# A mixture-of-experts block whose one weight buffer in the arena is loaded behind attention, with tile 0 routed and gathered ahead of tile 1

## The reference

```
t  = moba_attention(x)                       # 8 heads of 128, with a relative bias
h1 = layer_norm(ALPHA * x + t, ln_g[0], ln_b[0])
logits = h1 @ w_router + b_router            # 32 experts
top_logit, top_e = top_k(logits, 4); gate = softmax(top_logit)
for each expert e, for the tokens that chose it:
    g, u = split(h1[tokens] @ w_gate_up[e] + b_gate_up[e])      # 1024 -> 2 x 1024
    act  = min(g, 7) * sigmoid(1.702 * min(g, 7)) * (clip(u, -7, 7) + 1)
    y[tokens] += gate * (act @ w_down[e] + b_down[e])           # 1024 -> 1024
x = layer_norm(ALPHA * h1 + y, ln_g[1], ln_b[1])
```

## Time and profile before

| | us |
|---|---|
| median of 3 runs (lowest, highest) | 1375.93 (1375.58, 1377.43) |
| the profiled execution, its own time | 1376.69 |
| its span | 1374.9 |
| mean granted clock of TensorE, share of full | 0.994 |
| TensorE busy | 1330.1 (97%) |
| VectorE, ScalarE, GpSimd busy | 441.2, 346.9, 49.6 |
| bytes moved by DMA | 484.17 MB, mean 352 GB/s |

### The profile page before, as it was taken

The page is one execution under the profiler, slowest core; times in us unless marked ns, Lnnn a source line. Parts: engine busy times, 40 slices in busy tenths (PEclk is TensorE's granted clock), DMA queues, the critical chain, the costliest instruction groups (busy, mean ns, idle before and its releaser), DMA issues.

```text
span 1374.9 us, 17056 instructions
## 1 busy us (share of the span) xinstructions
PE 1330.1 (97%) x7358; PEld 718.6 (52%) x7358; DVE 441.2 (32%) x746; ACT 346.9 (25%) x576; POOL 49.6 (4%) x60
## 2 busy tenths in 40 slices
PE   9999999999999999969999999999999999999997
PEld 7996333333333333323333333333336998999986
DVE  5565121112111111101211111111107776888854
ACT  4541011101101110100110101100116545666642
POOL 2010000000000000000000000000002000022200
PEclk9999999999999999989999999999999999999999
DMA  9968999999999999999999999999996444265530
GB/s 378 376 233 359 428 421 430 430 432 429 430 431 430 430 431 429 431 429 430 431 432 429 432 429 431 429 431 430 432 427 242 153 154 153 87 254 183 184 123 31
DMA packets 44378, 484.17 MB, mean 352 GB/s; under 512 B 4780, under 2 KB 4832, under 8 KB 13712
## 3 DMA queue, kind: packets, MB, share of 16 engines
q1 hardware_dynamic: 42432, 477.63, 83.4%
q0 software_dynamic: 1872, 5.44, 1.1%
HBM read 481.99 MB, written 1.06 MB: 351 GB/s over the span
## 4 chain that ended last, share of the span: by engine, by line
PE 78%; DMA 15%; DVE 4%; issue 1%; ACT 1%; DVEq 0%; SPq 0%; ACTq 0%
PE bank L835 25%; PE bank L641 19%; PE bank L843 13%; DMA ring<-in_moe_w_gate_up 12%; PE bank L1143 4%; PE bank L855 3%; PE bank L808 3%; PE bank L624 3%; DMA ring<-in_w_in 2%; PE bank L827 2%; PE bank L751 2%; PE bank L1079 1%; PE bank L1029 1%; DMA arena<-in_x_by_feature 1%; DVE w_split L1552 1%
## 5 line engine op out<-in xcount | busy, mean ns | idle before, releaser
L835 PE MATMUL bank<-ring,arena 128*64 128x512 f32 x2048 | 448.9, 594 | 9.8 <-DMA ring<-in_moe_w_gate_up 9.8
L835 PEld LDWEIGHTS bank<-ring,arena 128*64 128x64 f32 x2048 | 143.2, 137 | 313.2 <-issue 290.3
L1750 DVE TENSOR_SCALAR arena<-bank 128x512 f32<-128x512 f32 x32 | 22.1, 692 | 654.8 <-PE bank L835 654.7
L843 PE MATMUL bank<-ring,arena 128*64 128x512 f32 x1008 | 223.5, 595 | 1.8 <-DMA ring<-in_moe_w_down 1.3
L641 PE MATMUL bank<-x_hi,w_split 128*128 128x256 f32 x1056 | 195.2, 285 | 2.1 <-DVE x_lo L1559 2.1
L641 PEld LDWEIGHTS bank<-x_hi,w_split 128*128 128x128 f32 x1056 | 167.2, 193 | 2.6 <-DVE x_lo L1559 1.5
L1552 DVE TENSOR_TENSOR w_split<-ring,w_split 128x2048 fp32r<-128x2048 f32 x61 | 139.5, 2289 | 60.4 <-ACT w_split L1198 60.2
L641 PE MATMUL bank<-x_lo,w_split 128*128 128x256 f32 x528 | 150.1, 284 | 0.0
L1299 ACT ACTIVATE arena<-arena 128x512 f32<-128x512 f32 x32 | 20.2, 630 | 495.3 <-DVE arena L1750 495.3
L843 PEld LDWEIGHTS bank<-ring,arena 128*64 128x64 f32 x1008 | 69.8, 137 | 135.3 <-issue 126.4
L1198 ACT CAST w_split<-ring 128x2048 fp32r<-128x2048 f32 x62 | 118.2, 1910 | 74.2 <-PE bank L641 42.5
(11 more groups left out here) (288 smaller groups left out, 1102.1 us busy)
## 6 DMA issues: line engine op xcount, KB each, us to landing
ring<-in_moe_w_gate_up SPq DMA_DIRECT2D x128, 2048.0 KB, 34.5
ring<-in_moe_w_down SPq DMA_DIRECT2D x63, 2048.0 KB, 34.1
ring<-in_ffn_w_up SPq DMA_DIRECT2D x22, 1024.0 KB, 4.8
ring<-in_w_in SPq DMA_DIRECT2D x14, 1024.0 KB, 8.0
ring<-in_ffn_w_down SPq DMA_DIRECT2D x11, 1024.0 KB, 4.9
ring<-in_a_w_in SPq DMA_DIRECT2D x10, 1024.0 KB, 20.9
ring<-in_a_w_out SPq DMA_DIRECT2D x2, 2048.0 KB, 14.0
ring<-in_w_out SPq DMA_DIRECT2D x4, 1024.0 KB, 5.0
```

The lines of the kernel that those rows point to most:

```text
L835: last = mm(bank[q // 2][half * 64:half * 64 + 64, :], chunk(xeT, c), w[:, c % 2, q * 512:(q + 1) * 512], start=False, stop=c == KC - 1)
L843: last = mm(bank[3][half * 64:half * 64 + 64, :], chunk(actT, c), w[:, c % 4, half * 512:(half + 1) * 512], start=c == 0, stop=c == KC - 1)
```

## The change

- SyncE issues piece 10 (`SPARE`) behind `o_ps` (attention's last product), ahead of the last four ring pieces, and no longer behind the norm.
- For that, the first norm's gain and offset move: `row_g0` to 13612, loaded by GpSimd right behind the relative bias; `row_b0` to 6144 (the place of attention's v), loaded behind `o_ps`, ahead of the router's weights. `bias_sel` moves to 13548, the output projection's fourth bank from 0 to 7, logits and ranks to banks 4 and 5.
- The norm's last step is done in two halves of 512 columns, each with its own `h1_ready`.
- TensorE computes tile 0's ranks as soon as tile 0 is chosen; VectorE makes tile 0's places and selection behind the PSUM copy of tile 1; TensorE gathers tile 0's half for expert 0 (`gather_first(0)`) behind tile 1's logits, and tile 1's half when its selection is ready.
- `add_bias` for expert 0 stands behind tile 0's logits, the tables stand behind the first gate-up piece of expert 0.
- Fillers: one pair of 512 columns more at tile 0, none at tile 1, and pairs of 256 columns (`fill`) in place of 512 around ranks and gather.

The diff, cut to its core:

```diff
@@ -162,7 +162,9 @@
...
         LEVEL_BANKS = (4, 6, 7, 4, 5, 6, 7, 4)
-        OUT_BANKS = (4, 6, 5, 0)
+        OUT_BANKS = (4, 6, 5, 7)
+        LOGITS = [bank[4][:, t * N_EXP:(t + 1) * N_EXP] for t in range(NT)]
+        RANKS = [bank[5][:, t * N_EXP:(t + 1) * N_EXP] for t in range(NT)]
         OUT_ORDER = (3, 0, 1, 2)
@@ -174,6 +176,7 @@
...
         moments = at(13542, NT, 2)
+        row_g0, row_b0 = at(13612, D), at(6144, D)
         row_g = at(8192, D)
@@ -189,7 +192,7 @@
...
         selgT = at(3456, NT, P)
-        bias_sel = at(3712, CAP)
+        bias_sel = at(13548, CAP)
         actT = at(6144, 4, P)
@@ -499,13 +502,13 @@
...
                 load_piece(A_OUT[g])
+            sp.wait_ge(o_ps, PAIRS)
+            load_piece(SPARE)
             for k, q in enumerate(OUT_ORDER):
...
             first_late = PIECES_E * (EXTRA_AFTER + 1)
-            sp.wait_ge(h1_ready, NT)
-            load_piece(SPARE)
             for n in range(SPARE + 1, first_late):
@@ -575,11 +578,10 @@
...
-            pool.wait_ge(max_ready, H)
-            pool.dma_start(row_g, row(ln_g[0, :], D)).then_inc(ln0_in, 16)
-            pool.dma_start(row_b, row(ln_b[0, :], D)).then_inc(ln0_in, 16)
+            pool.dma_start(row_g0, row(ln_g[0, :], D)).then_inc(rel_in, 16)
             pool.wait_ge(pt_ps, H)
             pool.wait_ge(o_ps, PAIRS)
+            pool.dma_start(row_b0, row(ln_b[0, :], D)).then_inc(ln0_in, 16)
             pool.dma_start(wr, w_router.rearrange("(c p) e -> p c e", p=P)).then_inc(moe_small_in, 16)
@@ -773,33 +775,60 @@
...
             before = const("before")
+            def add_bias():
...
+            def gather_first(t):
+                for half in range(2):
+                    last = mm(bank[2][half * 64:half * 64 + 64, :], sel[:, t, :], h1[:, t, half * 512:(half + 1) * 512],
+                              start=t == 0, stop=t == NT - 1)
+                return last
+            def fill():
+                mm(bank[3][:, 0:T], ident, cst[:, 0:T], start=True, stop=True)
             for t in range(NT):
-                pe.wait_ge(h1_ready, t + 1)
                 for g in range(2):
+                    pe.wait_ge(h1_ready, 2 * t + g + 1)
                     b = 4 + 2 * t + g
...
                 if t:
+                    pe.wait_ge(chosen_ready, 1)
+                    mm(RANKS[0], before, chosen[:, 0, :], start=True, stop=True).then_inc(rank_ps, 1)
+                    pe.wait_ge(h1T_dve, 1)
+                else:
                     repeat(3, 1)
-                    pe.wait_ge(h1T_dve, 1)
+                    pe.wait_ge(moe_small_in, 6 * 16)
                 pe.wait_ge(h1T_act, 2 + t)
-                if t == 0:
-                    pe.wait_ge(moe_small_in, 6 * 16)
                 for c in range(KC):
-                    last = mm(bank[1 + t][:, 0:N_EXP], h1T[:, c, t * P:(t + 1) * P], wr[:, c, :],
+                    last = mm(LOGITS[t], h1T[:, c, t * P:(t + 1) * P], wr[:, c, :],
                               start=c == 0, stop=c == KC - 1)
...
                 if t == 0:
+                    pe.wait_ge(bsel_ready, 1)
+                    add_bias()
                     repeat(3, 1)
-            pe.wait_ge(chosen_ready, 1)
-            mm(bank[0][:, 0:N_EXP], before, chosen[:, 0, :], start=True, stop=True)
-            mm(bank[0][:, N_EXP:2 * N_EXP], ones, chosen[:, 0, :], start=True, stop=False)
-            repeat(3, 1)
+            pe.wait_ge(sel_ready, 1)
+            gather_first(0)
+            mm(RANKS[1], ones, chosen[:, 0, :], start=True, stop=False)
+            fill()
             pe.wait_ge(chosen_ready, 2)
-            mm(bank[0][:, N_EXP:2 * N_EXP], before, chosen[:, 1, :], start=False, stop=True).then_inc(rank_ps, 1)
-            repeat(3, 1)
+            mm(RANKS[1], before, chosen[:, 1, :], start=False, stop=True).then_inc(rank_ps, 1)
+            fill()
+            pe.wait_ge(sel_ready, 2)
+            gather_first(1).then_inc(xe_ps, 1)
+            fill()
@@ -856,18 +878,20 @@
...
-            pe.wait_ge(sel_ready, 1)
-            gather().then_inc(xe_ps, 1)
...
             pe.wait_ge(xe_ready, 1)
             turn_chunks(2, xe, 2).then_inc(xeT_ps, 1)
+            fill()
+            def tables():
+                pe.wait_ge(gates_ready, 1)
+                for t in range(NT):
+                    turn(bank[3][0:N_EXP, t * P:(t + 1) * P], gates[:, t, :])
+                for t in range(NT):
+                    turn(bank[3][0:N_EXP, T + t * P:T + (t + 1) * P], place[:, t, :])
+                for t in range(NT):
+                    last = mm(bank[4][0:N_EXP, 0:1], chosen[:, t, :], ones[:, 0:1], start=t == 0, stop=t == NT - 1)
+                last.then_inc(table_ps, 1)
@@ -878,15 +902,17 @@
...
             for i in range(N_EXP):
-                pe.wait_ge(bsel_ready, i + 1)
                 if i:
+                    pe.wait_ge(bsel_ready, i + 1)
                     pe.wait_ge(selgT_ready, i)
-                add_bias()
+                    add_bias()
                 pe.wait_ge(xeT_ready, i + 1)
...
                     gate_up(s, buffer_of(n, 2)).then_inc(piece_done, 1)
+                    if i == 0 and s == 0:
+                        tables()
@@ -900,7 +926,7 @@
...
                 if i + 1 < N_EXP and not pause:
-                    pe.wait_ge(sel_ready, i + 2)
+                    pe.wait_ge(sel_ready, i + 3)
                     gather().then_inc(xe_ps, 1)
@@ -1649,12 +1675,12 @@
...
-            dve.wait_ge(ln0_in, 32)
+            dve.wait_ge(rel_in, 80)
             dve.wait_ge(x_in, 32)
...
                 dve.wait_ge(logit_ps, t + 1)
-                link(tt(logit[:, t, :], bank[1 + t][:, 0:N_EXP], br, ALU.add))
+                link(tt(logit[:, t, :], LOGITS[t], br, ALU.add))
                 link(dve.max(top8[:, t, :], logit[:, t, :]))
@@ -1666,6 +1692,10 @@
...
+            def select_bias(i):
+                ts(bias_sel, ones[:, 0:CAP], const("own")[:, i:i + 1], None, ALU.mult).then_inc(bsel_ready, 1)
+            select_bias(0)
             for t in range(NT):
@@ -1675,23 +1705,31 @@
...
                 root_of(t, moments[:, t, 1:2], 1.0, LN_EPS)
-                link(stt(h1[:, t, :], h1[:, t, :], moments[:, t, 0:1], row_g, ALU.subtract, ALU.mult))
+                link(stt(h1[:, t, :], h1[:, t, :], moments[:, t, 0:1], row_g0, ALU.subtract, ALU.mult))
                 r = refine(t)
-                stt(h1[:, t, :], h1[:, t, :], r, row_b, ALU.mult, ALU.add).then_inc(h1_ready, 1)
+                dve.wait_ge(ln0_in, 16)
+                for g in range(2):
+                    cols = slice(g * 512, (g + 1) * 512)
+                    stt(h1[:, t, cols], h1[:, t, cols], r, row_b0[:, cols], ALU.mult, ALU.add).then_inc(h1_ready, 1)
+            places = const("slot")
+            def first_places(t):
+                dve.wait_ge(rank_ps, t + 1)
+                link(stt(place[:, t, :], RANKS[t], 0.5, chosen[:, t, :], ALU.add, ALU.mult))
+                ts(sel[:, t, :], places[:, 0:CAP], place[:, t, 0:1], None, ALU.is_equal).then_inc(sel_ready, 1)
             choose(0)
...
             dve.tensor_copy(h1T[:, 4:8, P:T], bank[7][:, :].rearrange("p (c n) -> p c n", c=4)).then_inc(h1T_dve, 1)
+            first_places(0)
             choose(1)
             dve.wait_ge(chosen_ready, 2)
-            places = const("slot")
+            first_places(1)
...
                    place[:, :, i:i + 1].to_broadcast([P, NT, CAP]), ALU.is_equal).then_inc(sel_ready, 1)
@@ -1699,10 +1737,6 @@
...
-            dve.wait_ge(rank_ps, 1)
-            link(stt(place.rearrange("p t e -> p (t e)"), bank[0][:, 0:2 * N_EXP], 0.5,
-                chosen.rearrange("p t e -> p (t e)"), ALU.add, ALU.mult))
-            select(0)
             dve.wait_ge(gexp_ready, 1)
@@ -1710,7 +1744,6 @@
...
             dve.wait_ge(gates_ready, 1)
-            select_bias(0)
```

23 lines of the change are left out of this document (6 added, 17 removed).

## The result

The changed kernel takes 1384.37 us (median of 4 runs, 1382.78 to 1384.98), beside 1375.76 (4 runs, 1375.56 to 1377.43) of the kernel before: ratio 1.0059, 95% interval 1.0044 to 1.0074. By the medians it is 8.6 us slower, where 1.7 us faster was forecast.

What follows compares the result with a forecast made beforehand. The expert weights' DMA stream bounds the kernel. Queue 3.8 us earlier, release 1.55 plus 0.16; the smaller, 1.7, decides: 1375.93 becomes 1374.2 us, eight in ten 1372.4 to 1376.2.

Steps and rivals of the forecast that it cites:

- Part 3: Small loads after attention: router's weights and expert biases land 0.6 to 1.8 us later, by 112 at most, in time.
- The rival of the clock: TensorE, 122 to 131 us: thinned fillers let its clock fall, 1.75 us per fall; two falls give 1377.7; chance 0.07.
- Part 2: Routing chain: expert 0 starts at 130.8, 1.55 us earlier, so the first recycled piece is released at 134.4.
- From there on the stream is as before: Weight stream behind the first recycled piece: continues unchanged, and all later stages follow it, 1.7 us earlier.
- The forecast's own rule: First recycled piece: starts when both queue (3.8 us earlier) and release (1.55 us earlier, plus 0.16) let it.
- the forecast's 1.7: Whole kernel: gain from the earlier release, 1.55 us plus 0.16 us lost before, the smaller of the two limits.
- 4.88 us, 134.4 + 4.88 = 139.3: in time: Second recycled piece: issued at 138.6, before it must follow the first by 4.88 us.
- The hole filled: Weight stream, 108 to 112 us: the arena's piece, 4.88 us of transfer, goes into the 5.0 us hole.
- The queue alone decides: Rival at the first recycled piece: the arena's piece held the stream; moving it gains 3.8 us, 1372.1; chance 0.13.
- Hidden anyway: Rival in the experts' stage: TensorE sets its end; only 0.8 us come out, 1375.1, or nothing, 1375.9; chance 0.15.
- the room of 2.9 us: VectorE before tile 1's second half arrives at 115.6: 2.9 us in hand, so row_b0 costs nothing until 112.8.
- The rival on row_b0: Norm's offset load lands after 112.8 and delays tile 1's norm; 3.5 us later gives 1376.3; chance 0.02.

Runs made afterwards that it cites:

- 1: Changed kernel, with SyncE issuing the arena's piece only when the router's weights, router's bias and expert biases have landed; 1375.91 us, ratio 0.9999.
- 2: Changed kernel with the arena's piece issued behind the second norm again, as before the change; 1376.01 us, ratio 1.0012.
- 3: Changed kernel with row_b0, router's weights and bias and expert biases issued on SyncE's queue ahead of the arena's piece, instead of by GpSimd; 1376.83 us, ratio 1.0005.
- 9: Changed kernel with the expert biases and router's bias issued early, behind the first norm's scale; arena's piece still at 100 us; 1376.61 us, ratio 1.0005.
- 11: Changed kernel with the five weight pieces behind attention each loaded as four transfers of 4 KB per partition instead of one of 16 KB; 1376.47 us, ratio 1.0006.
- 5: Kernel before with only the arena's piece moved behind attention's last output pair, and the first norm's rows in their new places; 1382.82 us, ratio 1.0046.
- the seventh: Kernel of 1 (arena's piece waits for the small loads) with one filler more behind tile 1's transposes; 1375.88 us, ratio 1.0001.
- 14: Changed kernel with expert 1's down-projection pieces 10 and 11 used in the other order; 1385.12 us, ratio 1.0076.
- the twelfth: Kernel before with expert 1's down-projection pieces 10 and 11 used in the other order; 1377.6 us over 11 runs, ratio 1.0032.
- The fourth: Changed kernel with nine filler pairs instead of one ahead of TensorE's wait for the small loads; 1382.02 us, ratio 1.0048.
- the sixth: Changed kernel with five fillers instead of one ahead of TensorE's wait for the small loads; 1382.32 us, ratio 1.0039.
- the eighteenth: Changed kernel with five fillers ahead of the wait for the small loads and one more behind tile 1's transposes; 1381.83 us, ratio 1.0034.
- 8: Kernel of the seventh with the tables behind the third piece of expert 0 instead of the first; 1375.72 us, ratio 0.9997.
- 10: Kernel of 9 with one filler more behind tile 1's transposes and the tables behind expert 0's third piece; 1375.61 us, ratio 0.9996.
- 13: Kernel of 10 with expert 1's down-projection pieces 10 and 11 used in the other order; 1374.17 us over 11 runs, ratio 0.9987.
- 16: Kernel of 10 without expert 0's scatter products, so its output lacks the first expert; 1374.94 us, ratio 0.9991.
- 17: The twelfth's kernel, unchanged, run again on another occasion; 1376.02 us, ratio 1.0004.
- the fifteenth: Kernel before without expert 0's scatter products, so its output lacks the first expert; 1375.80 us, ratio 1.0002.

## Why the prediction was wrong

**The step that failed** is in Part 3: "The router's weights and the expert biases move back by 0.6 to 1.8 us to at most 112". I priced a wait of the issuing engine and took the landing from the earlier trace rows as it was. But that load of 6.9 us, and those of before (8.0 and 7.3), stood beside a single piece; the hole from 108 to 112, which I filled with weights, was the time in which the small loads got through. Beside a full queue they took 12.7 to 17.3 us, and the last landed at 120.9, not at 112. Experiments 1, 2, 3, 9 and 11 each take away the meeting of the two, in five ways, and each gives the 8 us back; 5 brings it about alone. That the queues take turns packet by packet is what the counts of 11 bear out. The Trainium skill (DMA: Bandwidth & Descriptors, "Queues, rings and completion order") says that each DMA engine goes round the queues that have work one whole packet at a time; the counts (177 to 174, 241 to 246) agree. I read the page for its fit of one load and passed over this rule, which spoke against the change.

**What the late landing cost**, by comparison with the seventh, which has the same order, no wait and a full clock: logits at 120.96 instead of 117.50, 3.5 us; from logits to expert 0 18.06 instead of 13.79, 4.3 us of halved clock; against that the new order's own gain, 131.29 instead of 132.28, 1.0 us. 3.5 + 4.3 - 1.0 = 6.7 (rounded). The rival of the clock, which had 0.07, so carries more than half; but I had it fall by thinned fillers, and here it fell behind a stop. All three profiles with such a stop (the changed kernel, 5 and 14; 3.7 to 5.2 us) have 0.50 behind it. The clock also falls without one: 0.50 at 126 to 128 in the first and second experiments, with no wait of TensorE above 0.3 us. Thinned fillers are not shown as the cause, since 3, 9 and 11 have the same order and kept 1.00, and the twelfth fell with before's fillers. The fourth, at full clock, bears the second share out with 13.63 us; the sixth and the eighteenth, which should have given the whole sum, did not keep the clock up.

**The release (Part 2) was nearly right, and what follows it was not.** With clock and loads in order expert 0 starts at 131.05 to 131.3 (experiments 7, 8, 10, 11 and 13; forecast 130.8), and the recycled piece goes out at 134.7 to 135.0 (134.4), 1.0 to 1.2 us sooner than before and not 1.55. The end should have come 1.7 us sooner. The second wrong step is "From there on the stream is as before": the forecast itself had TensorE only 0.8 us ahead behind the tables, and took it that the next release would be in time all the same.

Three times from each profile (expert 0's first matmul, an issue looked at below, the end of in_w_in) and the bytes that SyncE's queue moved from 95 to 150 us, put against before at 430 GB/s:

| kernel | expert 0 | issue | difference | MB | ahead by 150 us | in_w_in landed | ahead there |
|---|---|---|---|---|---|---|---|
| before | 132.28 | 186.48 | 54.20 | 18.43 | | 1031.59 | |
| changed | 139.02 | 194.13 | 55.11 | 15.47 | -6.9 | 1039.15 | -7.6 |
| 1 | 132.70 | 187.81 | 55.11 | 18.22 | -0.5 | 1032.78 | -1.2 |
| 5 | 138.79 | 192.99 | 54.20 | 15.78 | -6.2 | 1037.85 | -6.3 |
| 7 | 131.29 | 186.40 | 55.11 | 18.30 | -0.3 | 1032.23 | -0.6 |
| 8 | 131.05 | 186.16 | 55.11 | 18.35 | -0.2 | 1032.09 | -0.5 |
| 10 | 131.16 | 186.26 | 55.10 | 19.06 | +1.5 | 1030.54 | +1.1 |
| 11 | 131.09 | 186.20 | 55.11 | 18.56 | +0.3 | 1033.91 | -2.3 |
| 13 | 131.25 | 182.93 | 51.68 | 19.06 | +1.5 | 1030.46 | +1.1 |
| 18 | 136.94 | 192.04 | 55.10 | 16.19 | -5.2 | 1036.94 | -5.4 |

What the stream has won or lost by 150 us is there at its end, within 0.7 us in this table but for the eleventh, which loses 2 us more between 184 and 204 us (the fourth and sixth, not in the table, lose 1.2 more). Why, I cannot explain. The forecast's own rule is that the later of queue and release decides. By it three cases come out, from one profile each:

- **The queue still decides** (7 and 8): the arena's piece waits for the small loads, the hole at 110 us stays, the DMA share is 0.9 or more from 114 to 144 us, and an earlier release finds the queue full. That fits the eighth's tables giving nothing.
- **The release decides** (10, 13 and 16): the hole is filled, the recycled piece goes out 1.0 to 1.1 us sooner, and in_w_in lands 0.9 to 1.1 us sooner. This is what is left of the forecast's 1.7.
- **The second release decides** (3 and 9, the change as planned but for the small loads): with the tables between the first two pieces the second recycled piece is issued 4.3 us behind the first, not 3.4 as in before and the tenth. With the 1.6 taken off, the ninth's in_w_in lands 1.3 us later than the tenth's, though expert 0 starts at the same time. The filler is the only other edit between them, and the clock is 1.00 in both there; the tables were not moved alone with the hole filled. In the forecast this step was "4.88 us, 134.4 + 4.88 = 139.3: in time".

**A place that looks like a bound and is not shown to be one.** Of expert 1's last two pieces the arena's gives no slot back, so the load into piece 11's slot waits until TensorE has used both. Before, its issue, the next one, and the stretch:
```profile
186.48 0.33 SPq L489 DMA_DIRECT2D ring<-in_moe_w_gate_up  x1
191.08 0.33 SPq L489 DMA_DIRECT2D ring<-in_moe_w_down  x1
```
```profile
186.00:188.00 2.00, 2.00 (x16) 0.54 (x14) 0.00 (x0) 0.58 (x1) 0.00 (x0) 1.00 0.94 301
```
SyncE's queue runs dry there (0.13 MB at 188 to 190 us). I took this load for what sets the end: the changed kernel's is 7.65 us late and its in_w_in 7.56, and from this issue to the landing it is 845 us within 1 in the unswapped profiles, the eleventh apart (847.7). Two things speak against it. The seventh, eighth and tenth issue it within 0.24 us of each other, yet the tenth's in_w_in lands 1.5 to 1.7 us sooner; the tenth and thirteenth issue it 3.3 us apart, and theirs land together. And the DMA engines are not idle: their share is 0.94 in the row above and 1.06 in the next, for GpSimd's loads for the second norm and the down biases, 1.2 MB that have to be moved at some time, take the room (0.67 MB at 188 to 190).

Experiments 12, 13 and 17 went past that load by an edit. The next one (piece 12's slot) is as late, about 191 us, and GpSimd's loads, whose wait the edit moves too, then fall behind it, with 0.45 and 0.61 MB in the two stretches from 190 to 194. In the thirteenth:
```profile
182.93 0.33 SPq L493 DMA_DIRECT2D ring<-in_moe_w_gate_up  x1
190.96 0.33 SPq L493 DMA_DIRECT2D ring<-in_moe_w_down  x1
```
```profile
190.00:192.00 2.00, 2.00 (x12) 0.61 (x10) 0.00 (x0) 0.00 (x0) 0.00 (x0) 1.00 0.95 326
```
The medians of ten and thirteen are 1.4 us apart, on two chips, but their intervals overlap, and their profiled executions took 1374.23 and 1374.17, both without the fall at 1050: there the swap gave nothing. What sets the medians apart stays open.

The distance from expert 0 to this issue is the same to 0.01 us within each order of the tables: 54.20 with them ahead of expert 0, 55.11 with them inside, 0.91 more, of which the tables themselves take 0.76. So expert 0's gain of 1.0 to 1.2 us is 0.1 to 0.3 at this issue. What fills these 54 us in before is read off the chain: TensorE's own products but for 2.8 us from 146.28, in which VectorE works on expert 0's activations; in the fifteenth VectorE's work on expert 1's stands there a second time.

**The other steps.** The hole filled: right. The queue alone decides (0.13): refuted by the tenth, whose queue has run dry by 134 us and which gains 1.1 us at in_w_in, not 3.8. Hidden anyway (0.15): the medians of the mended versions come near it, between 0.6 us sooner and 1.0 later than those of before except the thirteenth's 2.1 sooner, but not for the reason given, since the tenth and thirteenth do bring the stream's end forward. row_b0: it landed at 111.3, 4 us later than forecast. VectorE waited 1.7 us for it and made it good in the room of 2.9 us that the forecast had named. The rival on row_b0 has its sum wrong: 3.5 us late against 1.55 won is 1.9 us slower, 1377.8, not 1376.3. The piece alone in the queue lands in 7.7, beside 7.8 in the earlier trace rows; the 6.8 us that the Trainium skill (DMA: Bandwidth & Descriptors, "Anatomy of one DMA") gives by its fit is for a load issued by GpSimd, which the forecast did not say, and the piece is SyncE's. The rule that the next piece must follow by 4.88 us was too lax: issued 4.35 us behind, at 147.06, it took 9.3 us, not 7.7.

## What to carry to other kernels

A hole in a DMA stream can be where small loads of another queue get through. Before filling it, list every load in flight beside it, with the time at which it is used, and send the small ones first, in smaller packets of the big ones, or long before. When a stream is bounded by the release of buffers, follow more than the first release: work moved behind it delays the second one, and here that took back what the first had won. And where one queue runs dry, look at the engines' share before calling it a hole, for another queue may be using them.

## What the runs showed of the hardware

- Two queues on the same DMA engines share by packets and not by bytes: 177 to 174 packets for 2.64 to 0.59 MB. A small load of 64 KB went from 7.3 to 17.3 us beside a full queue, and took 12.9 beside the same bytes in quarters.
- A stop of TensorE of 3.7 us ahead of 120.96 cost 4.3 us more by the clock. And the clock fell with TensorE busy the whole stretch, but in small products: sixth experiment, granted clock 0.50 at 130 to 134 us at a busy time of 2.00 in 2.00, after 1.36 in the stretch of 2 us at 126.
- A fall of the clock can belong to the execution and not to the kernel. Experiments 12 and 17 are one kernel: 0.50 at 126 to 128 us in the one profile and 1.00 in the other, 1.1 us at expert 0. The fall at 1050 us costs 1.4 us in seven of twenty profiles, one at 20 to 30 us costs 1.6 in two.
- The same instructions between expert 0 and a load 54 us later took the same time to 0.01 us in twelve profiles of different runs and chips (55.10 or 55.11), though two of these had started 1.6 us late.
